# A prefix pass in front of a gated-linear-attention trunk: unmodulated activations with folded weights, and a new order of pieces

## The reference, cut to what matters

```python
mod = (c @ w_mod + b_mod)[:, None, :]                    # one vector per sequence
sh1, sc1, g1, sh2, sc2, g2 = jnp.split(mod, 6, axis=-1)
h = rmsnorm(x, norm1_g) * (1 + sc1) + sh1                # D_MODEL = 1024
z = h @ w_in                                             # q, k, v, g, a, conv and merge gates
la = log_sigmoid(a @ w_alpha + b_alpha) / 16             # a: 16 columns; la: 4 heads x 128
S_t = diag(exp(la_t)) S_{t-1} + k_t^T v_t                # GLA state, per head 128 x 256
o_t = q_t S_t
...                                                      # gates, causal conv, w_o, SwiGLU, final norm
```

## Time and profile before

| | value |
|---|---|
| median of 3 runs | 1426.08 us (1425.94 to 1426.65) |
| profiled execution, its own time | 1425.53 us |
| its span, slowest core (core 1) | 1424.0 us |
| spans of the 8 cores | 1419.1 to 1424.0 us |
| busy: PE, DVE, ACT, POOL | 1322.3, 677.9, 504.8, 110.1 us |
| mean granted TensorE clock, core 1 | 0.972 |
| transfers | 96.97 MB |

### The profile page before, as it was taken

How to read it: one execution, slowest core, us unless ns; L and a number is a source line. 1 busy time by engine, 2 the same in 40 slices (tenths; PEclk the granted TensorE clock), 3 DMA queues, 4 the chain that set the end, 5 groups by cost and what they waited for, 6 DMA issues and landing times.

```text
span 1424.0 us, 22418 instructions; the slowest of 8 cores (1419.1 to 1424.0 us)
## 1 busy us (share of the span) xinstructions
PE 1322.3 (93%) x7524; PEld 686.9 (48%) x7524; DVE 677.9 (48%) x1240; ACT 504.8 (35%) x1122; POOL 110.1 (8%) x208
## 2 busy tenths in 40 slices
PE   1577999998989899999999999999999999999997
PEld 1233444444545455554445555555555445555443
DVE  1466656643656576652223335952222552222487
ACT  1576456332445555431212114971111001111233
POOL 3000100001000000011111210010000002000000
PEclk9778999999999999999999999999999999999999
DMA  9835301303222222263544566442322007232222
GB/s 175 214 119 156 53 1 23 67 1 60 57 45 38 38 46 38 45 106 45 74 60 72 78 102 159 133 75 31 45 31 45 0 1 111 31 45 30 60 104 111
DMA packets 60236, 96.97 MB, mean 68 GB/s; under 512 B 22646, under 2 KB 25606, under 8 KB 60124
## 3 DMA queue, kind: packets, MB, share of 16 engines
q0 software_dynamic: 29264, 53.02, 24.9%
q1 hardware_dynamic: 30860, 42.52, 9.8%
HBM read 133.95 MB, written 10.25 MB: 101 GB/s over the span
## 4 chain that ended last, share of the span: by engine, by line
PE 72%; ACT 9%; DVE 8%; issue 6%; DMA 4%; POOL 0%; DVEq 0%; ACTq 0%; POOLq 0%
PE psum L468 71%; ACT sb_arena L451 5%; DVE sb_arena L454 3%; DMA sb_wring<-wfm 2%; ACT sb_tmpB L451 2%; PE psum L471 2%; DVE sb_arena L462 2%; DVE sb_tmpB L462 1%; DMA sb_wring<-w_in 1%; DVE sb_arena L458 1%; ACT sb_rstd L451 1%; DVE sb_arena L459 0%; DVEq L171 0%; POOL sb_wring L437 0%; ACT sb_rstdo L451 0%
## 5 line engine op out<-in xcount | busy, mean ns | idle before, releaser
L468 PE MATMUL psum<-sb_arena,sb_wring 128*128 128x384 bf16 (+3 forms) x4448 | 835.8, 346 | 11.8 <-DVE sb_arena L465 7.2
L468 PEld LDWEIGHTS psum<-sb_arena,sb_wring 128*128 128x128 bf16 x4448 | 430.4, 98 | 385.8 <-issue 43.7
L468 PE MATMUL psum<-sb_wring,sb_arena 128*128 128x512 bf16 (+2 forms) x1596 | 349.8, 377 | 4.0 <-DMA sb_wring<-w_in 4.0
L451 ACT ACTIVATE sb_tmpB<-psum 128x384 f32<-128x384 f32 (+1 forms) x264 | 139.8, 533 | 593.0 <-PE psum L468 564.1
L454 DVE TENSOR_TENSOR sb_arena<-psum,sb_tmpB 128x384 bf16<-128x384 f32 (+5 forms) x254 | 148.2, 586 | 324.7 <-PE psum L468 299.6
L468 PEld LDWEIGHTS psum<-sb_wring,sb_arena 128*128 128x128 bf16 (+1 forms) x1596 | 155.8, 99 | 182.9 <-issue 6.4
L437 POOL DMA_DIRECT2D sb_wring<-wfm x140 | 75.6, 548 | 869.6 <-PE psum L468 730.4
L454 DVE TENSOR_TENSOR sb_tmpB<-psum,sb_tmpB 128x384 f32<-128x384 f32 (+2 forms) x80 | 47.8, 597 | 166.4 <-PE psum L468 166.2
L454 DVE TENSOR_TENSOR sb_arena<-psum,sb_arena 128x512 f32<-128x512 f32 (+2 forms) x106 | 72.6, 685 | 35.7 <-PE psum L468 35.1
L451 ACT ACTIVATE sb_arena<-sb_arena 128x1024 bf16<-128x1024 f32 (+2 forms) x60 | 60.5, 1010 | 74.3 <-DVE sb_arena L454 60.8
L451 ACT ACTIVATE sb_arena<-psum,sb_modT 128x128 bf16<-128x128 bf16 (+3 forms) x138 | 58.1, 500 | 54.6 <-PE psum L471 30.2
(11 more groups left out here) (94 smaller groups left out, 561.5 us busy)
## 6 DMA issues: line engine op xcount, KB each, us to landing
sb_wring<-wfm POOLq DMA_DIRECT2D x140, 256.0 KB, 7.7
sb_arena<-xm SPq DMA_DIRECT2D x29, 512.0 KB, 6.8
sb_arena<-xp SPq DMA_DIRECT2D x16, 512.0 KB, 11.8
ym<-sb_arena SPq DMA_DIRECT2D x16, 512.0 KB, 2.6
sb_wring<-w_ffn_out POOLq DMA_DIRECT2D x22, 256.0 KB, 4.5
sb_wring<-w_in POOLq DMA_DIRECT2D x16, 256.0 KB, 9.4
sb_wring<-w_mod POOLq DMA_DIRECT2D x16, 256.0 KB, 8.4
sb_wring<-w_o POOLq DMA_DIRECT2D x8, 256.0 KB, 9.3
```

Of the source, the lines that this page charges most:

```text
L451: return P.op("act", lambda e: e.activation(out=out, in_=in_, func=func, **kw), reads=reads, writes=writes)
L468: return P.op("pe", lambda e: e.matmul(out, lhsT=lhsT, rhs=rhs, start=start, stop=stop), reads=reads, writes=writes)
```

## The change

- The prefix's `norm_b` pieces no longer modulate: one eviction of both chunks (1024 columns) copies the transposed rows, on DVE, for blocks 0 and 1 on ACT in every second piece. For the own rows all modulating evictions are on DVE, but those of the first piece of block 4.
- `fold_a` and `fold_h` multiply `wa` (into a copy `wam`) and the four `wk` blocks (in place) by the scale, and compute `wa` and `wk` times the shift (`ba`, `bk`), which are added at the evictions. `wk` is loaded a second time for the own rows. `halo` makes the two modulated halo rows.
- The host reverses the prefix rows. The scan then carries on from block to block (`car`), and column 0 of `bcP` holds the carried sum, so the decay of a key is the Exp of `bcP` alone: one Exp in place over four heads and 512 columns. The Ln takes two heads at a time, and the first head's scan is issued two pieces later.
- `pre_ktm`'s copies move from DVE to ACT.
- norm_a(0), norm_t(0), norm_a(1) and norm_t(1) are put among the 16 md blocks. Row loads wait only for their buffers, but those of block 1 for md block 3 and those of block 2 for md block 15.
- The steps' order is written out as a string of letters. Norm_a's multiplies of block s+2 move into step s. The pieces of `pre_state` begin in step 4, so that two are left after the loop instead of seven.

```diff
-        for c_ in (1536, 512, 1024):
+        for c_ in (0, 512, 1024, 1536):
...
+                if i < NPB:
+                    o_, i_ = dst[:, kp * 2:kp * 2 + 2, 0:512], psb(b).rearrange("p (k c) -> p k c", k=2)
+                    dr = [dregs[kp * 2], dregs[kp * 2 + 1]]
+                    if i < 2 and kp % 2:
+                        act(o_, i_, AF.Copy, [r_ps[b]], dr)
+                    else:
+                        cp(o_, i_, [r_ps[b]], dr)
+                    yield
+                    continue
...
-                        if kp == 0 or (kp == 2 and i % 2):
+                        if kp == 0 and i < NPB + 1:
...
+        def fold_a():
+            cp(shb, modT[:, 0, :, 0], [r_modT[0]], [r_shb])
+            tt(wam, wa[:], modT[:, 1, :, 0:1].broadcast_to([128, KT, 16]), ALU.mult, [r_wa, r_modT[1]], [r_wam])
+            b = newbank()
+            for k in range(KT):
+                mm(psf(b)[0:16, 0:1], wa[:, k, :], shb[:, k:k + 1], k == 0, k == KT - 1, [r_wa, r_shb], [r_ps[b]])
+            cp(ba[0:16, :], psf(b)[0:16, 0:1], [r_ps[b]], [r_ba])
+
+        def fold_h(h, wk):
+            b = newbank()
+            for k in range(KT):
+                mm(psf(b)[:, 0:1], wk[h].lhs(k), shb[:, k:k + 1], k == 0, k == KT - 1, [wk[h].reg, r_shb], [r_ps[b]])
+            cp(bk[:, h:h + 1], psf(b)[:, 0:1], [r_ps[b]], [r_bk])
+            wr = wring[:, wk[h].s, :].rearrange("p (k d) -> p k d", k=KT)
+            tt(wr, wr, modT[:, 1, :, 0:1].broadcast_to([128, KT, 128]), ALU.mult, [wk[h].reg, r_modT[1]], [wk[h].reg])
...
-            cp(aTp[:, st, :], psf(b)[0:16, :], [r_ps[b]], [r_aTp[st]])
+            ts(aTp[:, st, :], psf(b)[0:16, :], ba[0:16, 0:1], None, ALU.add, None, [r_ps[b], r_ba], [r_aTp[st]])
+            cp(bcP[st][:, :, 0:1], car[:].unsqueeze(2), [r_car], r_bcP[st])
...
+                if h % 2:
+                    act(tmpB[:, h - 1:h + 1, :], tmpB[:, h - 1:h + 1, :], AF.Ln, ...)
+                if h >= 2:
+                    scan(h - 2)
...
-                act(tmpB[:, ti, :], bcP[st][:, h, :], AF.Exp, [r_bcP[st][h], r_nbP[st]], [r_tmpB[ti]], scale=1.0 / 16, bias=nbP[:, st, h:h + 1])
-                tt(kdP[st][:, h, :], psf(b), tmpB[:, ti, :], ALU.mult, [r_ps[b], r_tmpB[ti]], [r_kdP[st][h]])
+            act(bcP[st][:, :, 0:512], bcP[st][:, :, 0:512], AF.Exp, r_bcP[st], r_bcP[st], scale=-1.0 / 16)
+                stt(kdP[st][:, h, :], psf(b), bk[:, h:h + 1], bcP[st][:, h, 0:512], ALU.add, ALU.mult, [r_ps[b], r_bk, r_bcP[st][h]], [r_kdP[st][h]])
...
-                cp(kdtmP[ki], psb(b)[:, 0:512], [r_ps[b]], [r_kdtmP[ki]])
+                act(kdtmP[ki], psb(b)[:, 0:512], AF.Copy, [r_ps[b]], [r_kdtmP[ki]])
...
+        begin(0, [])
+        take(md, 4)
+        run(nas[0])
+        begin(1, [mdregs[3]])
+        take(md, 4)
+        run(norm_t(0))
+        take(md, 4)
+        run(nas[1])
+        take(md, 3)
+        run(norm_t(1))
+        run(md)
...          # wk loads, then:
+        begin(2, [mdregs[15]])
+        begin(3, [])
+        fold_a()
+        run(gates[0])
+        for h in range(NH):
+            fold_h(h, wk)
+        halo()
+        take(nas[2], 5)
+        for s_ in range(0, NBK - 2):
+            go("GKGGGGKKKSSGkTTTnkkkTnnn" if s_ == 0 else "KkGSSnkKnGGKGGGKTnkkTTnTn" if s_ < NPB else "kkkSknCSnnCTCTTTnnCC",
+               S=scaled(s_ + 2),                                    # norm_a's multiplies, then the loads of block s+4
+               K=pre_keys(s_, wk) if s_ < NPB else none,
+               G=gates[s_ + 1],
+               k=pre_ktm(s_ - 1) if 0 <= s_ - 1 < NPB else none,
+               C=itertools.islice(state, 5) if s_ >= NPB else none,
+               T=norm_t(s_ + 2),
+               n=itertools.islice(nas[s_ + 3], len(blk_tiles(s_ + 3)) + 1) if s_ + 3 < NBK else none)
+        held.clear()
+        wk = [wfm("k", h, [r_hT[0][2]]) for h in range(NH)]
...
-        m["xp"] = np.ascontiguousarray(xseq[0:half_tok])
+        m["xp"] = np.ascontiguousarray(xseq[0:half_tok][::-1])
```

More of the change, by code:

```diff
@@ L390, in build @@
         rstd = sb("rstd", (128, 16)); r_rstd = [Reg("rstd%d" % i) for i in range(4)]
-        nbP = sb("nbP", (128, 2, 4)); r_nbP = [Reg("nbP%d" % i) for i in range(2)]
+        car = sb("car", (128, NH)); r_car = Reg("car")
         ksum = sb("ksum", (128, 4)); r_ksum = Reg("ksum")
@@ L660, in norm_t @@
             if i < NPB:
[L661 removed]
+                return norm_b(i, hTp[i % 4], r_hTp[i % 4], 0)
             g = i - NPB
@@ L680, in pre_gate, with scan @@
+            cp(bcP[st][:, :, 0:1], car[:].unsqueeze(2), [r_car], r_bcP[st])
             yield
+            def scan(h):
+                P.op("dve", lambda e: e.tensor_tensor_scan(out=bcP[st][:, h, 1:513], data0=consts[:, 1:2].broadcast_to([128, 512]), data1=tmpB[:, h, :],
+                                                           initial=car[:, h:h + 1], op0=ALU.mult, op1=ALU.add),
+                     reads=[r_consts, r_tmpB[h], r_car], writes=[r_bcP[st][h]])
             for h in range(NH):
-                ti = rot("tmpB", NT4)
@@ L696, in pre_gate @@
+            scan(3)
+            cp(car[:].unsqueeze(2), bcP[st][:, :, 512:513], r_bcP[st], [r_car])
             yield
@@ L1208, in ffn2_gen, with begin, take @@
                 final(16)
-        run(norm_a(0))
+        NBK = NPB + NG
+        nas = [None] * NBK
+        def begin(i, after):
+            if i < NBK and nas[i] is None:
+                nas[i] = norm_a(i, after)
+                next(nas[i])
+        begin(0, [])
+        md = mod_fm_gen([(0, 0, 0), (1, 1, 1)])
+        def take(g, n):
+            return run(itertools.islice(g, n))
+        take(md, 4)
+        run(nas[0])
         dma("pool", wa[:], wa_d.rearrange("p (k c) -> p k c", c=16), [], [r_wa])
         dma("pool", walpha[:], w_alpha[:, :], [], [r_walpha])
-        run(mod_fm_gen([(0, 0, 0), (1, 1, 1)]))
+        begin(1, [mdregs[3]])
[6 more added lines that the diff above has]
+        run(md)
         wk = []
@@ L1219, in build @@
             wk.append(u)
-        NBK = NPB + NG
-        nas = [None] * NBK
-        def begin(i):
-            if i < NBK and nas[i] is None:
-                nas[i] = norm_a(i, ldafter[0])
-                next(nas[i])
-                ldafter[0] = [r_xin[xlast[0]]]
-        ldafter = [[mdregs[11]]]
-        begin(1)
-        begin(2)
-        run(norm_t(0))
-        cp(hT[:, :, TM:TX], hTp[0][:, :, 510:512], r_hTp[0], [r_hTh])
-        spread([(pre_gate(0), 6), (nas[1], 7)])
-        state = pre_state()
@@ new lines, in build, with go, scaled @@
+        begin(3, [])
+        state = pre_state()
+        gates = [pre_gate(pb) for pb in range(NPB)] + [iter(())] * NBK
+        fold_a()
+        run(gates[0])
+        def go(order, **gens):
+            for c in order:
+                next(gens[c], None)
+            for c in gens:
+                run(gens[c])
+        def scaled(i):
+            next(nas[i], None)
+            yield
+            run(nas[i])
+            begin(i + 2, [])
+            yield
+        for h in range(NH):
+            fold_h(h, wk)
```

60 lines of the change are left out of this document (26 added, 34 removed).

## The result

The changed kernel takes 1401.46 us (median of four runs, 1399.6 to 1401.62), the kernel before 1426.37 beside it: a ratio of 0.9815, 95% interval 0.9803 to 0.9827. The profiled execution took 1399.6 us; its slowest core, core 1, has a span of 1398.1, 25.9 us less than the 1424.0 before. This is the page of it, busy tenths in 40 slices, and its two queues; it answers to the earlier trace rows.

A forecast was written before the change was run, and what follows sets the result against it. It took transfers to bound stage 1, waits between engines steps 0 to 3, TensorE the rest. 6.8 us by the loop's end plus 6.45 after made 13.2 off the 1424.0 us span, so a 1413 us median, range 1402 to 1425.

The forecast's parts named there:

- A step of the loop: Steps 0 to 3: three engines at 14.2 to 14.6 us, 8% allowed, 15.9 us a step, together 59.7 us.
- Steps 4 to 6: Last loop steps: state pieces, transposes and ktm on TensorE, 36.1 us, with 6% allowed 38.3 us.
- After the loop: Behind the loop: five state pieces (9.45 us) already done, less 3 us for gate_h(0), so 6.45 us gained.
- Everything fits: Rival, chance 0.14: rows use slack in stage 1 (5.4 us less), 8% and 6% allowances vanish (6.6 less): 1401 us.
- Hidden: Stage 1: norm_t(0), norm_a(1) and norm_t(1) cost nothing under the md weights; their 64 transposes take 5 us.
- slower: Rival, chance 0.12: TensorE stays at half clock; gain used up at mean clock 0.71 over steps 0 to 3; 1433 at 0.65.
- The clock stays: Rival, chance 0.18: short, frequent waits keep TensorE's clock at 0.77 over steps 0 to 3, 67.5 us instead of 59.7: 1421 us.

## Why the prediction was right or wrong

**The main mechanism was right, the size was half.** A written order that takes the waits off TensorE, and state pieces moved into the loop, are what the runs show as the gain. Two other parts of its chain, the early rows and the folding where it stands, bought nothing that the runs can tell from zero. 24.9 us came where 13 were forecast. The spans differ by 12.7 us: 1.0 at the start of step 0, 4.7 in "A step of the loop", 5.5 in "Steps 4 to 6", and 1.45 in "After the loop".

**The failed step** is the sum of the loop, 59.7 + 38.3 us, where 55.0 + 32.8 were measured: 10.2 of the 12.7 us. Step by step:

| | forecast, us | measured, us |
|---|---|---|
| step 0 | 16 | 16.3 |
| step 1 | 15.9 | 16.4 |
| step 2 | 15.9 | 14.1 |
| step 3 | 11.9 | 8.2 |
| steps 4 to 6 | 38.3 | 32.8 |

Steps 0 and 1, in which the clock was low, took a little longer than forecast. All that was missed lies behind them, at full clock. The allowances for waits make 6.6 of the 10.2 us (4.4 in steps 0 to 3, 2.2 in steps 4 to 6), the prices of the work the other 3.6, nearly all in steps 4 to 6. Of step 3's 3.7 us, some 1.9 are its first key group, which TensorE did within step 2 (111.25 us, above), while the forecast counted it in step 3. The forecast's 11.9 is also 11% over its 10.7 and not 8%; by 8% it is 11.6.

**First part: prices of chains.** It priced eight matmuls of 512 columns at the 1.89 us of the earlier trace rows, and eight transposes at 0.62. Both hold the last one's latency, which the next group hides. The changed kernel's timeline has the long groups:

```profile
126.16 1.89 PE L477 MATMUL psum<-sb_arena 128*128 128x512 bf16 x8
...
128.89 7.07 PE L477 MATMUL psum<-sb_arena 128*128 128x512 bf16 x32
```

```profile
109.02 2.40 PE L480 MATMUL psum<-sb_identb,sb_arena 128*128 128x128 bf16 x40
```

(7.07 - 1.89) / 24 = 0.216 us for one matmul more, 1.73 for eight; (2.40 - 0.62) / 32 = 0.056 for a transpose, 0.45 for eight. By these a step's 32 + 8 + 4 matmuls of 512 columns and 48 transposes are 44 x 0.216 + 48 x 0.056 = 12.2 us where the prediction had 14.2. The step with three added matmuls per group gave 12.8, so that changing from one short group to the next costs some 0.6 more. In steps 1 and 2 this over-pricing made no difference to the forecast, which went by VectorE's 14.6 us as the fullest engine. In steps 4 to 6, where TensorE is the fullest, it did: the 15 state pieces are 15 x 8 x 0.216 = 25.9 us where it had 28.4, and the 96 transposes some 5.4 where it had 7.7. The same holds in small on VectorE and ScalarE, where an operation starts 0.07 to 0.1 us before the one ahead has ended: VectorE's 14.6 us for a step were 13.5 in step 2. Part of that is the copy of 1024 columns, priced at 0.75 between two bounds:

```profile
99.18 2.48 DVE L474 COPY sb_arena<-psum 128x1024 bf16<-128x1024 bf16 x4
```

0.60 to 0.62 us each. Here the Trainium skill's figure (VectorE: DVE Perf Modes, "The TRN2 errata"), from which the prediction had worked out an estimate of 0.66, was nearer than the value taken, and the trace agrees with it within a tenth.

**Second part: the allowances.** It added 8% to steps 1 to 3 and 6% to steps 4 to 6. Step 2 took 14.1 us with VectorE busy 13.51: 4% by its own busy time. From 113.3 to 154.3 us TensorE was busy 40.55 of 41.0, so steps 3 to 6 had hardly any slack. 8% was cut from the old order's 17%, an average over steps in which the order itself made the waits; the old order says nothing about the new one's.

**"Everything fits" gave the number, not the reasons.** This rival said 1401. Half of it was that the rows cost nothing in stage 1; they cost 4.8 us, near the main forecast's 5.4. That forecast's 47.0 us for the last md matmul (47.71 measured) was met in part by luck: "Hidden" was wrong for norm_t(1)'s transposes, which stood in TensorE's queue in front of it. The other half, the 6.6 us of allowances, is what the loop as a whole gained, though steps 0 and 1 kept theirs. What made up for the first half was the 3.6 us of over-pricing, 1.45 us behind the loop and 1.0 us in front of it, which no case had.

**The clock.** It fell as feared in step 0, 0.71, and the 24 key matmuls there take 8.18 us where the kernel without folding needs 5.35 for the same; it comes into that step with TensorE busier (12.81 of the 18.8 us from 47.7 on, against 11.50). With filler matmuls they take 5.36. The "slower" rival wanted 0.71 as the mean over steps 0 to 3. But step 1 had 0.92 and step 2 1.00, 0.89 over the four: the clock came back while TensorE was busy for 16.26 of step 1's 16.4 us. "The clock stays" (0.77) failed by the same rows. The order that was undone stood at 0.82 over 66 to 130 us, with the gaps, so low clock and gaps stand together; the runs don't divide the 20 us between them.

**The parts, by the runs.** The written order with the state move is worth some 20 of the 25 us when added to the old kernel. Taken out of the changed one, the order costs 20.5 and the state move 4.5. The 6.45 of "After the loop" is not the price of that move, since it leaves out what the pieces cost in step 4. Folding is worth nothing in the place it was given, and 5 to 6 us once the folds lie in VectorE's idle time. The prediction did price the folds (5.4 us on the path; measured 4.9), but did not ask whether they could stand elsewhere. "After the loop" charged 3 us to gate_h(0); the gaps there are 1.38 and 0.57 us.

**What stays open.** How the order's gain divides over its joints. Breaking one (S and T in front) costs 23.6 us, mending one in the old order gives 2 at most. The worth is not additive, and the runs don't split it further. No run undoes the carried scan, the Exp in place or the Ln of two heads, so what they are worth is not known. Whether filler matmuls help the changed kernel isn't settled either.

## What to carry to other kernels

With three in-order engines near balance the order of issue was the largest lever here: find in the trace the reader that stands directly behind its producer in program order, and put independent work between them that takes as long as the producer does. Do it at every joint, since one that was broken again took back the whole gain. Before work is called hidden, look at what stands behind it in the same engine's queue. Price chains by start-to-start spacing from the longest groups in the timeline, never by short groups' durations, and don't carry the old order's slack into the new one. Before weights are prepared on an engine in front of a stage, look for that engine's idle time behind its next wait.

## What the runs showed of the hardware

- Moving four row tiles in beside the weight blocks delayed the last weight block by 4.8 us (40.9 to 45.7, means of eight cores, without transposes in between) of the 6.9 us that the tiles take: the two queues share the DMA engines. This agrees with the round-robin rule of the Trainium skill (DMA: Bandwidth & Descriptors, "Queues, rings and completion order") and not with a weights' queue that is served first; that the turns go packet by packet no run here shows.
- A matmul of 512 columns at full clock adds 0.216 us to a chain and a transpose 0.056, while the recorded groups of eight show 1.89 and 0.62. At half clock 32 transposes take 3.59 us.
- A TensorE gap of 4.7 us is followed by eight matmuls in 3.57 us instead of 1.89, one of 5.5 us by 29 transposes in 3.25, half clock in both cases: on top of the gap comes slower work.
- Work doubled on VectorE and ScalarE came through to the end at 0.87 and 0.81 by the medians, added work on TensorE at 0.53. In a step at full clock with TensorE shown busy for 13.5 of 14.1 us, 2.6 us more made it 1.3 us longer, until it was busy for 15.39 of 15.39: the recorded busy time of TensorE overstated here how full it was, by some 0.7 us.
- One multiply of 128x1024 bf16 by a broadcast scale took 1.21 to 1.23 us on VectorE from SBUF, as long as the 1.214 from PSUM.
